# Every panel of seven products in block 1 opens with the two products that need no weight sums

## The chip, the cores and the metric

The kernel runs on one core of a Trainium2 chip. The metric is the time of one execution on the device in microseconds (us), as the median of several executions. All data are float32.

## The reference, cut to what matters

The reference chains two blocks over 256 tokens of width 1024. Block 1 has two layers; each is a hybrid mixer and a SwiGLU network. Block 2 (a gated recurrence, a retention mixer and two expert layers) is not touched by the change.

```
for l in range(2):
    proj = x @ w_in[l]            # 1024 x 6912: a_q a_k a_v | b_h b_b b_c | c_q c_k c_v | g_a g_b g_c
    y_a = sliding_window_attention(a_q, a_k, a_v)      # 8 heads of 64
    y_b = b_b * short_conv(b_c * b_h)
    y_c = moba_attention(c_q, c_k, c_v)                # 8 heads of 64, one block of 256 keys
    merged = sigmoid(g_a) * (y_a @ w_br_a) + sigmoid(g_b) * (y_b @ w_br_b) + sigmoid(g_c) * (y_c @ w_br_c)
    x = layer_norm(ALPHA * x + merged @ w_out)
    x = layer_norm(ALPHA * x + (silu(x @ w_gate) * (x @ w_up)) @ w_down)
```

## The kernel before, in words

**Panels.** The projections and the two up-projections of the feed-forward network are cut into panels of 1024 x 512 weights. A ring of six slots in SBUF receives them; SyncE (SP) issues the loads, each of which waits until TensorE has finished with the panel that held the slot. Each layer has 24 panels (`SEVENS`) that are multiplied by the x of 1024 x 256 with Strassen's scheme in Winograd's form: seven products of half-size blocks in place of eight.

**The seven products.** They are numbered 1 to 7. Products 1 and 2 read weights and x as they are. Products 5, 6 and 3 need sums of weight blocks (s1, s2, s4), and product 7 a difference that is written back into the panel; product 4 needs only sums of x, which are made once for many panels. VectorE makes the four sums in `weight_sums` (L2683, L2685, L2687, L2688). The three buffers for s1, s2, s4 exist once, so `weight_sums(q)` first waits until product 3 of panel q-1 is through (L2677: one semaphore step is given after product 3, L2331). For the first panel of the feed-forward run and the first gate panels after the first attention this wait is another one or none.

**PSUM.** The products go in pairs to four banks: A holds 5 and 6, B holds 3 and 7, C holds 1 and 2, D holds 4. `product_banks(q)` gives the order in which TensorE opens and fills them, the planner (`BankPlan`) numbers them, and VectorE waits for them. In panels 0, 4, 7, 9, 11 and 13 (`RUNS`, the first panels of runs) the order is C, A, B, D; in the other 18 it is A, B, C, D. Banks are handed out in turn: seven while one is held for the adaptive modulation's rows (up to the seventh feed-forward panel), then eight. A unit of work opens its bank as soon as the unit that used it before has emptied it.

**The combination.** ScalarE copies product 1 to SBUF (`first_product`, L2554) once bank C is full and the bank C before it is empty. VectorE then waits for that copy and all four banks and combines them in seven instructions (`parts`, L2699 to L2706). L2700 frees bank A, L2704 bank B, L2705 bank C and L2706 bank D.

**Order of work.** Each engine runs one list written by hand. TensorE in a layer: x transposed; panels 0 to 3 (b_h, b_b, b_c, a_q); a_k and a_v; eight scores (L2361, L2362); panels 4 to 6 (cq, ck, cv); eight scores; panels 7 and 8 (g_b); transposes and values of the first attention (L2246, L2406); the branch projection (L2263); panels 9 and 10 (g_a) and a branch; panels 11 and 12 (g_c), the second attention's values and a branch; the out projection (L2443); panels 13 to 23 (feed-forward); the down projection (L2501, L2509). VectorE, wherever it can, makes the sums of panel q+1 ahead of the combination of panel q. Between them stand logits (L2813), normalisations, the feed-forward product (L3009), and `ada_sums` (L2760, L2763), in which VectorE multiplies modulation weights. After panel 22 it makes the sums of the hidden rows (L3016 to L3019) and the first sums of the down weights (L3031 to L3034), and then combines panel 23.

Of the kernel before, what the change touches and what calls it, by code (L numbers as in the profile page):

```python
# [115 lines left out]
def view(ap, *dims):  # L116

    names = "abcd"[:len(dims)]
    return ap.rearrange(f"p ({' '.join(names)}) -> p {' '.join(names)}", **dict(zip(names[1:], dims[1:])))
# [10 lines left out]

FIRST = {"b": 0, "aq": 3, "cq": 4, "ck": 5, "cv": 6, "gb": 7, "ga": 9, "gc": 11, "ff": 13}
SEVENS = FIRST["ff"] + PAIRS
RUNS = (0, 4, 7, 9, 11, 13)


def product_banks(q):

    banks = (("A", (5, 6)), ("B", (3, 7)), ("C", (1, 2)), ("D", (4,)))
    return [banks[i] for i in (2, 0, 1, 3)] if q in RUNS else banks


STREAMS = 2
# [1721 lines left out]
def program(nc, I, K, out):  # L1864

    banks = BankPlan()
# [8 lines left out]
    def sevens(q, count=1):  # L1875
        steps = []
        for n in range(q, q + count):
            for name, _ in product_banks(n):
                steps += [("sv", n, name)] + [BankPlan.TICK] * (name == "A")
            steps += [R]  # L1880
        return steps
# [3 lines left out]

    layer = [(BankPlan.HOLD, BANKS - 1, ("adaG",))] + [("xT", t, m) for t in range(TT) for m in range(2)]
    layer += sevens(FIRST["b"]) + [("par",)] + sevens(FIRST["b"] + 1, 3)
    layer += [("ak",), ("av",), R, EV] + [("sa", h) for h in range(HEADS)]
    layer += sevens(FIRST["cq"]) + sevens(FIRST["ck"]) + [EV] + sevens(FIRST["cv"]) + [("sc", h) for h in range(HEADS)]
    layer += sevens(FIRST["gb"], 2) + attend("a") + branch("b") + [EV]  # L1890
    layer += sevens(FIRST["ga"], 2) + branch("a") + [EV]
    layer += sevens(FIRST["gc"], 2) + attend("c") + branch("c") + [EV]
# [19 lines left out]
    with ctx:  # L1912
# [72 lines left out]
        def middle(q):  # L1985
            return [view(a, 2, P) for a in M_PLACES[phase(q)]]
# [14 lines left out]
        def quarter_of(q, r, t):  # L2001

            if q == FIRST["cv"]:
                return view(cv[:, t, :], 2, 2, P)[:, :, r, :]
            return tiles_of(q)[:, :, r, P * t:P * t + P]
# [68 lines left out]
        def open_bank(pe, stage, key, i=0):  # L2074

            b = banks.bank(stage, key)
            pe.wait_ge(bank_free[b], banks.free(stage, key, i))
            return psum[:, b, :]

        def full_bank(eng, stage, key, i=0):  # L2080

            eng.wait_ge(pe_done, banks.full(stage, key, i))
            b = banks.bank(stage, key)
            return psum[:, b, :], bank_free[b]

        def wait_emptied(eng, stage, key, i=0):

            eng.wait_ge(bank_free[banks.bank(stage, key)], banks.emptied(stage, key, i))
# [142 lines left out]
        def _(pe):  # L2231
# [3 lines left out]
            def panel(i, width):  # L2235

                n = state["panel"]
                state["panel"] += 1
                per = state.get("per", 0)
                pe.wait_ge(panel_in[n % RING], i * (32 * per // RING) + 32 * (n // RING + 1))  # L2240
                return view(ring[:, n % RING, :], PANEL // width, width)
# [12 lines left out]
            for l in range(DEPTH):  # L2254
# [37 lines left out]
                def factor_pair(q, c, k, u, slot):  # L2292

                    w = view(slot[:, 4 * (c in (2, 4)) + k, :], 2, 2, P)[:, :, 1 if c in (4, 7) else 0, :]
                    left_made, right_made = left_sums(q), right_sums(q)
                    left = left_made[c][:, k] if c in left_made else w
                    if q != FIRST["cv"]:
                        left = left[:, u, :]
                    if c in right_made:
                        return left, right_made[c][:, k, :]  # L2300
                    return left, xT[:, 4 * (c in (2, 3)) + k, P * (c in (3, 5)):P * (c in (3, 5)) + P]

                def seven_products(q):

                    if q == 0 and l == 0:
                        pe.wait_ge(first_half_in, 16)
                        slot = view(ring[:, 0, :], KT, HALF)
                        state["panel"] += 1
                    else:
                        slot = panel(l, HALF)  # L2310
                    for name, two in product_banks(q):
                        bank = open_bank(pe, "layer", ("sv", q, name), l)
                        for j, c in enumerate(two):
                            if q == 0 and l == 0 and c == 2:
                                pe.wait_ge(panel_in[0], 32)
                            if c in (5, 6, 3, 7):
                                pe.wait_ge(sums_ready, 4 * (l * SEVENS + q) + {5: 1, 6: 2, 3: 3, 7: 4}[c])
                            if q == 0 and c in (5, 6, 7, 4):
                                pe.wait_ge(x_sums_ready, 8 * l + {5: 1, 6: 2, 7: 3, 4: 4}[c])
                            if q == FIRST["ff"] and c in (7, 5, 6, 4):  # L2320
                                pe.wait_ge(x_sums_ready, 8 * l + {7: 5, 5: 6, 6: 7, 4: 8}[c])
                            for k in range(4 if q == FIRST["cv"] else 0):
                                left, right = factor_pair(q, c, k, 0, slot)
                                last = mm(view(bank[:, SEQ * j:SEQ * j + SEQ], 2, P), right, left, start=k == 0, stop=k == 3)
                            for u in range(0 if q == FIRST["cv"] else 2):
                                for k in range(4):
                                    left, right = factor_pair(q, c, k, u, slot)
                                    a = SEQ * j + P * u
                                    last = mm(bank[:, a:a + P], left, right, start=k == 0, stop=k == 3)  # L2329
                            if c == 3:  # L2330
                                last.then_inc(pe_done, 1)  # L2331
                        last.then_inc(pe_done, 1)

                seven_products(FIRST["b"])
                pe.wait_ge(par_loaded, 4 * 16)
                pe.wait_ge(par_rest_loaded, 4 * 16)
                bank = open_bank(pe, "layer", ("par",), l)
                nc.tensor.transpose(bank[:, 0:128], par_rows, ident)
                nc.tensor.transpose(bank[:, 128:216], par2_rows[0:88, :], ident[0:88, 0:88]).then_inc(pe_done, 1)
                seven_products(FIRST["b"] + 1)  # L2340
                seven_products(FIRST["b"] + 2)
                seven_products(FIRST["aq"])

# [306 lines left out]
        def _(dve):  # L2650
# [16 lines left out]
            for l in range(DEPTH):  # L2667
# [22 lines left out]
                def parts(q):  # L2690

                    dve.wait_ge(first_ready, l * SEVENS + q + 1)
                    part, freed = {}, {}
                    for name, two in product_banks(q):
                        bank, freed[name] = full_bank(dve, "layer", ("sv", q, name), l)
                        for j, m in enumerate(two):
                            part[m] = view(bank[:, SEQ * j:SEQ * j + SEQ], 2, P)
                    one, sum_16, sum_165 = middle(q)
                    step(TTo(sum_16, one, part[6], ALU.add))  # L2699
                    TTo(sum_165, sum_16, part[5], ALU.add).then_inc(freed["A"], 1)  # L2700
                    wait_emptied(dve, "layer", ("sv", q, "A"), l)
                    TTo(quarter_of(q, 1, 1), sum_165, part[7], ALU.add)
                    step(TTo(sum_16, sum_16, part[7], ALU.add))
                    TTo(quarter_of(q, 0, 1), sum_165, part[3], ALU.add).then_inc(freed["B"], 1)  # L2704
                    TTo(quarter_of(q, 0, 0), one, part[2], ALU.add).then_inc(freed["C"], 1)  # L2705
                    TTo(quarter_of(q, 1, 0), sum_16, part[4], ALU.subtract).then_inc(freed["D"], 1)  # L2706
# [67 lines left out]
                step(V.tensor_copy(mods_0[:, :, :], mods_now[:, :, :]))  # L2774
                weight_sums(1)
                parts(0)
                bank, freed = full_bank(dve, "layer", ("par",), l)
                V.tensor_copy(par[:, :], bank[:, 0:128])
# [3 lines left out]
                step(V.tensor_copy(conv_w[:, :, :], view(par2[:, 64 + l * 12:76 + l * 12], 3, 4)))  # L2782
                weight_sums(2)
                parts(1)
                dve.wait_ge(cT_ready, l + 1)
                ada_sums(0, 0, 4)
                weight_sums(FIRST["aq"])
                parts(2)
                ada_sums(0, 4, KT)
                weight_sums(FIRST["cq"])  # L2790
# [368 lines left out]
```

## Time and profile before

| | |
|---|---|
| median of 3 executions | 2484.89 us (2484.7 to 2488.94) |
| profiled execution | 2485.11 us, span 2483.3 us |
| mean granted clock of TensorE | 0.961 of full |
| TensorE busy | 2188.5 us, 88% |
| VectorE busy | 1245.6 us, 50% |
| ScalarE busy | 369.2 us, 15% |

A view's busy time is the time in which an engine has at least one instruction in flight. A releaser (behind "<-") is the instruction that ended an idle time, as inferred from semaphores.

### The profile page before, as it was taken

What the parts mean: (1) busy time and instruction counts of PE and PEld (TensorE: products, weight loads), DVE (VectorE), ACT (ScalarE), POOL (GpSimd) and SP (SyncE); (2) the same over time, 40 slices, a digit from 0 to 9 for tenths busy, and PEclk for the clock granted to TensorE, in tenths of its full rate; (3) what the DMA queues carried; (4) which work ended last, traced back from release to release, by engine and by line L of the source; (5) the groups of instructions that cost most, each with busy time, mean ns of one, the idle gap of its engine ahead of it and who ended that gap; (6) DMA issues with size and microseconds to landing.
All of it is one profiled execution on the core that took longest, in us unless ns stands there. A gap on an engine that the chain in (4) does not pass through costs nothing.

```text
span 2483.3 us, 43563 instructions
## 1 busy us (share of the span) xinstructions
PE 2188.5 (88%) x19414; PEld 1578.0 (64%) x19414; DVE 1245.6 (50%) x2209; ACT 369.2 (15%) x825; POOL 38.5 (2%) x69
## 2 busy tenths in 40 slices
PE   8999999999999999999999988887799986565655
PEld 8998798499988984746545645454588543232322
DVE  7987787689777785926632222121444631111111
ACT  1121101012111001144430000000201420000000
POOL 0000000000000010000000000000000000000000
PEclk9999999999999999999999999999999998878787
DMA  9655765475558555401428999999920289999996
GB/s 321 238 170 187 247 195 221 155 269 207 190 192 276 191 205 189 161 28 35 160 104 333 426 426 426 426 426 426 366 102 34 95 339 426 426 428 426 428 427 289
DMA packets 168444, 659.16 MB, mean 265 GB/s; under 512 B 8358, under 2 KB 55970, under 8 KB 143554
## 3 DMA queue, kind: packets, MB, share of 16 engines
q1 hardware_dynamic: 162576, 639.66, 66.1%
q0 software_dynamic: 5312, 16.57, 2.1%
q8 instruction: 153, 2.51, 0.4%
q14 instruction: 33, 0.27, 0.0%
q10 hardware_dynamic: 370, 0.15, 0.0%
HBM read 655.12 MB, written 1.23 MB: 264 GB/s over the span
## 4 chain that ended last, share of the span: by engine, by line
PE 59%; DMA 28%; DVE 9%; ACT 2%; issue 1%; DVEq 0%; SPq 0%; ACTq 0%
PE psum L2329 20%; DMA ring<-in_moe_w_up 9%; DMA ring<-in_moe_w_gate 9%; DMA ring<-in_moe_w_down 9%; PE psum L789 5%; PE psum L538 4%; PE psum L2501 4%; PE psum L2263 3%; PE psum L715 3%; PE psum L806 2%; PE psum L2443 2%; PE psum L603 2%; PE psum L601 2%; PE psum L2509 1%; PE psum L859 1%
## 5 line engine op out<-in xcount | busy, mean ns | idle before, releaser
L789 PE MATMUL psum<-ring,arena 128*32 128x256 f32 x5888 | 383.1, 416 | 162.1 <-DMA ring<-in_moe_w_up 83.1
L789 PEld LDWEIGHTS psum<-ring,arena 128*32 128x32 f32 x5888 | 207.8, 118 | 334.3 <-issue 142.8
L1653 DVE TENSOR_TENSOR arena<-psum,spare 32x512 f32<-32x512 f32 (+1 forms) x128 | 70.9, 554 | 364.3 <-PE psum L806 363.0
L806 PE MATMUL psum<-ring,lnp 128*32 128x256 f32 x3072 | 192.5, 405 | 67.6 <-DMA ring<-in_moe_w_down 63.1
L806 PEld LDWEIGHTS psum<-ring,lnp 128*32 128x32 f32 x3072 | 103.6, 115 | 154.0 <-DMA ring<-in_moe_w_down 48.5
L1642 DVE TENSOR_TENSOR lnp<-arena,psum 128x512 f32<-128x512 f32 (+1 forms) x32 | 26.1, 816 | 326.4 <-PE psum L789 326.4
L2329 PE MATMUL psum<-ht,ring 128*128 128x128 f32 x1472 | 175.9, 278 | 2.3 <-DMA ring<-in_w_in 2.3
L2329 PEld LDWEIGHTS psum<-ht,ring 128*128 128x128 f32 x1472 | 170.8, 195 | 7.0 <-issue 7.0
L538 PE MATMUL psum<-ring,ht 128*128 128x512 f32 x320 | 140.6, 595 | 0.0
L1096 ACT ACTIVATE arena<-psum 128x512 f32<-128x512 f32 (+1 forms) x32 | 15.7, 491 | 669.2 <-PE psum L789 669.2
L2763 DVE SCALAR_TENSOR_TENSOR spare<-ring,arena,spare 128x512 f32<-128x512 f32 x168 | 113.8, 743 | 0.0
L538 PEld LDWEIGHTS psum<-ring,ht 128*128 128x128 f32 x320 | 59.9, 190 | 72.7 <-issue 72.5
L2329 PE MATMUL psum<-lnp,ring 128*128 128x128 f32 x768 | 92.0, 275 | 0.0
L2329 PEld LDWEIGHTS psum<-lnp,ring 128*128 128x128 f32 x768 | 88.8, 192 | 0.0
L2329 PE MATMUL psum<-c,ring 128*128 128x128 f32 x704 | 85.5, 275 | 0.0
L2263 PE MATMUL psum<-arena,ring 128*128 128x256 f32 x384 | 84.3, 380 | 0.9 <-ACT arena L2538 0.9
L2329 PEld LDWEIGHTS psum<-c,ring 128*128 128x128 f32 x704 | 82.0, 192 | 0.0
L2263 PEld LDWEIGHTS psum<-arena,ring 128*128 128x128 f32 x384 | 72.5, 190 | 11.4 <-ACT arena L2538 1.4
L715 PE MATMUL psum<-ring,arena 128*128 128x512 f32 x160 | 70.3, 594 | 1.8 <-DVE arena L1530 0.9
L2683 DVE TENSOR_TENSOR ht<-ring 128x1024 f32<-128x1024 f32 x39 | 47.7, 1223 | 45.4 <-PE psum L2329 44.1
L2329 PE MATMUL psum<-lnp,ht 128*128 128x128 f32 x512 | 60.0, 275 | 0.0
L2501 PE MATMUL psum<-ring,arena 128*128 128x512 f32 x128 | 57.7, 593 | 1.3 <-DVE arena L3034 1.3
(544 smaller groups left out, 3207.6 us busy)
## 6 DMA issues: line engine op xcount, KB each, us to landing
ring<-in_moe_w_down SPq DMA_DIRECT2D x64, 2048.0 KB
ring<-in_moe_w_gate SPq DMA_DIRECT2D x62, 2048.0 KB
ring<-in_moe_w_up SPq DMA_DIRECT2D x60, 2048.0 KB
ring<-in_w_in SPq DMA_DIRECT2D x51, 1024.0 KB, 8.9
ring<-in_ada_w SPq DMA_DIRECT2D x48, 1024.0 KB
ring<-in_w_ffn_gate SPq DMA_DIRECT2D x22, 1024.0 KB
ring<-in_w_ffn_up SPq DMA_DIRECT2D x22, 1024.0 KB
ring<-in_w_ffn_down SPq DMA_DIRECT2D x20, 1024.0 KB
```

The costliest lines, as they stand in the source:

```text
L538: last = mm(bank, lhs[:, k, P * t:P * t + P], slot[:, k, :], start=k == 0, stop=k == KT - 1)
L601: last = mm(out, left[:, part, :], right, start=k == 0, stop=k == 3)
L603: last = mm(out, right[:, P * part:P * part + P], left, start=k == 0, stop=k == 3)
L715: last = mm(bank, lhs[:, k, a:a + P], slots[n][:, k, :], start=k == 0, stop=k == KT - 1)
L789: last = mm(bank[32 * j:32 * j + 32, SPLIT * m:SPLIT * m + SPLIT], (x_last if layer else x_four)[:, k, e % 4, SLOTS * m:SLOTS * m + SLOTS] ...
L806: last = mm(bank[32 * j:32 * j + 32, SPLIT * m:SPLIT * m + SPLIT], hidT[:, e % 2, a:a + 32], slot[:, f % 4, SPLIT * j:SPLIT * j + SPLIT], ...
L1653: ins = TTo(y_four[32 * q:32 * q + 32, s0:, cols], view(bank[r, 0:width], len(src), SPLIT), gb_moe[r, s0:, cols], ALU.mult)
L2263: last = mm(bank[:, SEQ * h:SEQ * h + SEQ], slot[:, k, P * (2 * m + h):P * (2 * m + h + 1)], rhs[:, k, :], start=k == 0, stop=k == k_tiles ...
L2329: last = mm(bank[:, a:a + P], left, right, start=k == 0, stop=k == 3)
L2443: last = mm(bank, left, right, start=k == 0, stop=k == 3)
L2501: last = mm(down[c], left, right, start=i == 0, stop=False)
L2763: ins = STT(out=acc, in0=slot[:, k, :], scalar=weight, in1=acc, op0=ALU.mult, op1=ALU.add)
```

## The change

`product_banks` no longer takes the panel's number. It gives C, A, B, D for all 24 panels of a layer. The planner, TensorE and VectorE all ask it, so the order of filling, the numbering of the banks and the waits change together. The instructions and their number are the same. Panels 1, 2, 3, 5, 6, 8, 10, 12 and 14 to 23 change their order.

```diff
-RUNS = (0, 4, 7, 9, 11, 13)
-def product_banks(q):
+def product_banks():
     banks = (("A", (5, 6)), ("B", (3, 7)), ("C", (1, 2)), ("D", (4,)))
-    return [banks[i] for i in (2, 0, 1, 3)] if q in RUNS else banks
+    return [banks[i] for i in (2, 0, 1, 3)]
...
     def sevens(q, count=1):
-            for name, _ in product_banks(n):
+            for name, _ in product_banks():
                 steps += [("sv", n, name)] + [BankPlan.TICK] * (name == "A")
...
                 def seven_products(q):
-                    for name, two in product_banks(q):
+                    for name, two in product_banks():
                         bank = open_bank(pe, "layer", ("sv", q, name), l)
...
                 def parts(q):
-                    for name, two in product_banks(q):
+                    for name, two in product_banks():
                         bank, freed[name] = full_bank(dve, "layer", ("sv", q, name), l)
```

## Rows read from the trace of the kernel before

**Rows 1.** The page's busy times: us, share of the span, instructions.
```profile
PE 2188.5 (88%) x19414; PEld 1578.0 (64%) x19414; DVE 1245.6 (50%) x2209; ACT 369.2 (15%) x825; POOL 38.5 (2%) x69
```
**Rows 2.** Waits of TensorE: engine, line, releaser: us in total, times, longest.
```profile
PE psum L2406 <- DVE arena L2704: 3.1, 4, 0.8
...
PE psum L2501 <- DVE arena L3034: 1.3, 2, 0.7
...
PE psum L2361 <- DVE arena L2813: 0.9, 2, 0.5
...
PE psum L2361 <- DVE arena L2704: 0.6, 2, 0.3
```
**Rows 3.** Timeline of TensorE, panel 1: start, us, what, [idle before <-releaser].
```profile
26.32 3.77 PE L2329 MATMUL psum<-lnp,ht 128*128 128x128 f32 x32
...
31.72 1.95 PE L2329 MATMUL psum<-lnp,ring 128*128 128x128 f32 x16
...
38.86 3.74 PE L2329 MATMUL psum<-lnp,ht 128*128 128x128 f32 x32
```
**Rows 4.** Timeline of VectorE, the sums and combinations of panels 1 to 3.
```profile
32.02 1.23 DVE L2683 TENSOR_TENSOR ht<-ring 128x1024 f32<-128x1024 f32 x1 [1.02 <-PE psum L2329]
...
39.16 0.42 DVE L2699 TENSOR_TENSOR c<-c,psum 128x256 f32<-128x256 f32 x1 [2.27 <-PE psum L2329]
...
46.63 1.21 DVE L2683 TENSOR_TENSOR ht<-ring 128x1024 f32<-128x1024 f32 x1
...
51.67 0.42 DVE L2699 TENSOR_TENSOR c<-c,psum 128x256 f32<-128x256 f32 x1 [0.17 <-PE psum L2329]
```
**Rows 5.** Timeline of VectorE behind panel cv.
```profile
108.11 1.22 DVE L2683 TENSOR_TENSOR ht<-ring 128x1024 f32<-128x1024 f32 x1
...
114.26 0.42 DVE L2699 TENSOR_TENSOR c<-c,psum 128x256 f32<-128x256 f32 x1 [1.28 <-PE psum L2324]
...
116.30 0.41 DVE L2705 TENSOR_TENSOR arena<-c,psum 128x256 f32<-128x256 f32 x1
```
**Rows 6.** Timeline of TensorE: cq's end, ck, cv, the scores, panel 7.
```profile
84.80 3.74 PE L2329 MATMUL psum<-lnp,ring 128*128 128x128 f32 x32
88.53 3.81 PE L2329 MATMUL psum<-lnp,ht 128*128 128x128 f32 x32
...
101.77 3.72 PE L2324 MATMUL psum<-ht,lnp 128*128 128x256 f32 x16
...
116.43 0.48 PE L2361 MATMUL psum<-arena 64*128 64x128 f32 x2 [0.32 <-DVE arena L2704]
...
118.41 3.84 PE L2329 MATMUL psum<-ht,ring 128*128 128x128 f32 x32
```
**Rows 7.** Timeline of VectorE: the combination of panel 8 begins.
```profile
143.84 0.41 DVE L2699 TENSOR_TENSOR c<-c,psum 128x256 f32<-128x256 f32 x1
```
**Rows 8.** Timeline of TensorE: four groups of transposes, then attention values.
```profile
143.52 1.78 PE L2246 MATMUL psum<-const,arena 128*128 128x128 f32 x12
146.09 0.66 PE L2406 MATMUL psum<-arena 128*64 128x256 f32 x4 [0.79 <-DVE arena L2704]
```
**Rows 9.** Timeline of VectorE, feed-forward: sums of panel 23, combination of panel 22.
```profile
405.25 1.23 DVE L2683 TENSOR_TENSOR ht<-ring 128x1024 f32<-128x1024 f32 x1 [1.10 <-PE psum L2329]
...
410.05 0.68 DVE L3009 TENSOR_TENSOR arena<-arena 128x512 f32<-128x512 f32 x1
412.43 0.42 DVE L2699 TENSOR_TENSOR arena<-arena,psum 128x256 f32<-128x256 f32 x1 [1.70 <-PE psum L2329]
```
**Rows 10.** Timeline of TensorE in block 2: its two longest waits near 1300 us.
```profile
1298.47 0.41 PE L2246 MATMUL psum<-const,arena 128*64 128x128 f32 x2 [2.31 <-DVE arena L1556]
...
1305.59 0.67 PE L739 MATMUL psum<-arena,const 64*128 64x256 f32 x2 [3.27 <-DVE arena L1576]
```
**Rows 11.** Windows of core 0: us, busy by engine (instructions), PEclk, DMA share, GB/s.
```profile
1296.00:1300.00 4.00, 1.69 (x6) 0.82 (x6) 2.67 (x13) 3.60 (x4) 0.00 (x0) 1.00 1.00 369
...
1308.00:1312.00 4.00, 4.00 (x28) 4.00 (x27) 0.03 (x1) 1.24 (x4) 0.00 (x0) 0.71 0.10 41
```

## The prediction

> **What bounds the kernel now.** I read the page first, then the waits of TensorE, then the timelines of TensorE and VectorE side by side in block 1, and last the stretches where the granted clock falls. The page's first part puts TensorE at 88% of the span [rows 1]; the question is what holds it up in block 1, because only there does the edit act. The waits answer: in the two layers of block 1, TensorE stands still for VectorE in a few places, and they are short [rows 2]: one score (L2361) waits for the logits that empty its bank, another for the combination of panel cv, the attention values (L2406) wait for a bank that the last gate panel's combination empties, and the down projection (L2501) waits for its first weight sums. No product of L2329 waits for VectorE. So block 1 is bound by TensorE's own work, with VectorE just behind it at a few seams. Removing waits can return next to nothing; delaying VectorE at a seam costs in full.
>
> **The measure of the panel.** A panel of seven products takes 38.86 − 26.32 = 12.54 us; 16 of its 112 matmul records are one product. From 26.32 to 31.72 run products 5, 6, 3; from 31.72 to 38.86 run 7, 1, 2, 4 in 7.14 us [rows 3], so one is 1.785 and two are 3.57 us. The weight sums of panel q+1 (L2683 to L2688) overwrite the buffer that products 5, 6, 3 of panel q read, so they wait for product 3 of q. In the order A, B, C, D product 3 is third; in C, A, B, D it is fifth. **This is the main effect: on 18 of 24 panels of each layer, VectorE may begin the next weight sums 3.57 us later.** What it gives back: the next product 5 always comes four products after product 3; today, behind a run's first panel, only two.
>
> **Steady state, cost nothing.** After product 3 the new order leaves products 7, 4 and the next 1, 2: 4 x 1.79 = 7.1 us. Sum s1 is there after about 0.3 (the wait: 31.72 to 32.02 [rows 3, 4]) + 1.25 us. In the feed-forward run VectorE does per panel: sums 4.80 (405.25 to 410.05), the product of L3009 0.7, the combination (7 instructions, L2699 to L2706) 2.7 [rows 9], and in four panels 2.7 of adaptive sums: 10.9 us of 12.5. So VectorE keeps pace and its combination merely slides: now it waits 1.70 us for the panel's last product [rows 9]; then it starts 3.57 − 1.70 = 1.87 us later, or 1.9 with the spacing of two instructions back to back. Banks: the panel's first bank is now C, freed by the sixth instruction (L2705) instead of A, freed by the second. With seven or eight banks the next panel's last product is the first to need it, 10.7 us after the previous panel's end; it is free 1.9 + 2.5 us after. Covered. What I cannot read is a C-first panel in steady flow. Bounds: a run's first pair, C behind other work, takes 3.84 us against 3.74 for the same 32 records elsewhere [rows 6], so 0.10 x 36 panels = +3.6 us at most; nothing at least, since the same instructions run. I take zero: the 0.10 stands where another kind of work precedes.
>
> **Seam 1, the sliding-window scores.** VectorE is loaded here by adaptive sums. Panel 1: sums for panel 2 move from 32.02 to 35.59; its combination waited 2.27 us, so it starts at 40.39 instead of 39.16, +1.23. The following sums (46.63, no wait) would slide to 47.86; they wait for product 3 of panel 2 until 38.86 + 5 x 1.785 + 0.3 = 48.1, and the next combination goes from 51.67 to 48.1 + 4.8 = 52.9, +1.2. From there to the logits VectorE has no wait left, so they start 1.2 later too [rows 4]. The eighth score needs the bank of the first logit; it waits 0.9 / 2 = 0.45 us already [rows 2], so TensorE slips **+1.2 us**. What hid it today was those 2.27 us; that cover is gone.
>
> **Seam 2, the scores of the second attention.** Panels cq and ck follow. Product 5 of ck starts at 88.53, 3.73 us after product 7 of cq (84.80), where two products would take 3.57 [rows 6]: it waits for s1. With C first that is gone: −0.16, and −0.1 that follows it. So cv starts at 101.77 + 0.95 = 102.72 [rows 6]. In cv product 3 now ends five products in (5 x 1.75 = 8.75), at 111.5, and the sums behind it start at 111.7 instead of 108.11 [rows 5]. They take 4.80, so the combination of cv starts at 116.5 instead of 114.26 (it had waited 1.28). Second effect: the fourth score takes cv's first bank. Today that is A, and the fifth is the one that stands, for B, until 116.43 [rows 6]; then it is C, whose reader L2705 starts 2.04 after the combination's start (116.30 − 114.26) and takes 0.41 [rows 5], so 118.95, and the score starts at 119.0. Five scores remain, at (118.41 − 116.43) / 4 = 0.495 each: the gate panel starts at 121.5 instead of 118.41. **+3.1 us in all, of which 2.1 are new at this seam.**
>
> **Seams 3 and 4, the attention values.** The combination of the second gate panel starts at 143.84 and frees bank C by L2705, 2.04 + 0.41 us later [rows 5, 7]: 146.29. The fourth transpose group takes this bank now; a group takes 1.78 / 4 = 0.445. It starts at 146.35 and the values at 146.8 instead of 146.09 [rows 8]: **+0.7 us**. Rows 2 count four such waits (two per layer), so +0.7 again behind gc. The combination itself isn't late here: only the second panel of each pair changes its order, nothing in VectorE's queue waits for its product 3 sooner than today, and it starts with product D.
>
> **Seam 5, the down projection.** The last sums of the run start at 405.25 + 3.57; the combination of panel 22 at 412.43 + 1.9; then follow, with no wait between, the hidden sums and the first down sums, for which L2501 already waits 1.3 / 2 = 0.65 us [rows 2]. So **+1.9 us**. Behind it the down sums are ahead of TensorE again.
>
> **Other queues.** SP's panel loads wait for a panel's last product, which stays D; so do GpSimd's. They move with TensorE. ScalarE's copy of product 1 comes earlier and still waits for the former C bank; no combination waits for it.
>
> **Sum.** 3.06 + 0.72 + 0.72 + 1.91 = 6.4 us per layer, 12.8 for two (rows 2 count each seam equally in both). The profiled execution took 2485.11 us, 1.8 more than its span of 2483.3; the median of three is 2484.89. So 2485.11 + 12.8 − 0.2 = **2497.7 us**, +0.5%. The second block has no such panels and its streams start as its first panels come free, so it passes the shift on.
>
> **The rivals.**
> *A, the clock falls (2501).* The wait in seam 2 grows from 0.3 to some 2.5 us (three scores run from 102.72 + 12.3 = 115.0 to 116.5; the fourth starts at 119.0). In the second block a wait of 2.31 leaves the granted clock full; one of 3.27 us is followed by a stretch at 0.71 [rows 10, 11], part of it at 1.2 GHz, about (1 − 0.71) x 4 = 1.2 us, to which I add 0.5 for what may lie in the slice before. With 1.7 per layer: 2497.7 + 3.4. For it: 2.5 lies between. Against: it is nearer to 2.31. [...]
> *B, only the down projection is late (2489).* If VectorE's slack in the attention stage is more than the timeline shows (waits are rounded by the wait's own latency), seams 1 to 4 stay and 2 x 1.9 remain: 2484.9 + 3.8 = 2488.7. Against: rows 4 and 5 leave no gaps.
> *C, not slower (2483).* Behind each of the six run heads, product 5 comes two products after product 3 today. If each of these hand-overs costs the 0.16 seen at ck, in places that the waits don't name, the four products of cover give back 12 x 0.16 = 1.9 us: 2483.0. It decides if VectorE's sums, not its combination, are what TensorE meets next; the price is read at 88.53. Against it: the sums at ck are late because of adaptive sums, and elsewhere [rows 3] product 5 follows without a gap.
> *D, nothing moves (2485).* The slides of 1.2 to 1.9 us all die in waits of VectorE. For it: in the feed-forward run they do. Against: the four seams are places where TensorE waits for VectorE already.
>
> **How the numbers follow.** Forecast 0.74 (own range 2493.5 to 2501); A 0.09; B 0.07; C 0.05; D 0.05. About 0.2% (5 us) is what a measurement here tells from no change. B, D lie inside it, C too but may go beyond if the panels shorten; so slower 0.84, same 0.12, faster 0.04. The range 2491 to 2502 holds the forecast with a smaller seam 2 below, and rival A or the 0.10 per panel above.
>
> **What would show it.** The wait of L2361 for L2813 grows to 1.7 us each, that of L2361 for the combination to some 2.5 with L2705 as its releaser; L2246 waits for L2705 about 1 us before the values; L2501 waits 2.6; L2683 starts 3.57 later on changed panels; the feed-forward panels stay at 12.5. It is wrong if the feed-forward panels change length, if the waits above stay as they are, or if time goes or comes outside block 1.

## The result, and the profile after

| | before | changed |
|---|---|---|
| median | 2485.52 us (4 executions, 2484.7 to 2488.9) | 2509.14 us (4 executions, 2506.05 to 2512.78) |
| ratio | | 1.0093, 95% interval 1.008 to 1.0106 |
| profiled execution, span | 2485.11, 2483.3 us | 2512.78, 2511.0 us |
| mean granted clock | 0.961 | 0.952 |

The change makes the kernel 0.9% slower, 23.6 us. The forecast was 12.8 us. Line numbers of the changed kernel are one lower than those of the kernel before (L2328 is L2329).

The waits of TensorE in the changed kernel, in the columns of [rows 2]:

```profile
PE psum L2245 <- DVE arena L2704: 6.7, 4, 1.7
...
PE psum L2500 <- DVE arena L3033: 5.2, 2, 2.6
...
PE psum L2360 <- DVE arena L2704: 4.9, 2, 2.5
...
PE psum L2360 <- DVE arena L2812: 3.3, 2, 1.7
```

These are the same places as before and no new one, and each wait has grown: in order 1.67 for 0.79, 2.60 for 0.65, 2.48 for 0.32, 1.67 for 0.46 us. Where the kernel before waited for L2704 before the values, the changed one waits for the former L2705 before the fourth transpose group (here L2245 and L2704), and it is the fourth score, not the fifth, that stands in the second attention. The growth adds up to 14.2 us over two layers.

VectorE, timeline, where [rows 4, 5, 9] stood:

```profile
34.61 1.23 DVE L2682 TENSOR_TENSOR ht<-ring 128x1024 f32<-128x1024 f32 x1 [4.59 <-PE psum L2328]
...
39.41 0.42 DVE L2698 TENSOR_TENSOR c<-c,psum 128x256 f32<-128x256 f32 x1
...
112.43 1.23 DVE L2682 TENSOR_TENSOR ht<-ring 128x1024 f32<-128x1024 f32 x1 [4.11 <-PE psum L2323]
...
117.23 0.42 DVE L2698 TENSOR_TENSOR c<-c,psum 128x256 f32<-128x256 f32 x1
...
414.00 1.23 DVE L2682 TENSOR_TENSOR ht<-ring 128x1024 f32<-128x1024 f32 x1 [2.76 <-PE psum L2328]
...
419.52 0.42 DVE L2698 TENSOR_TENSOR arena<-arena,psum 128x256 f32<-128x256 f32 x1
```

The idle time has changed sides. Before, VectorE waited ahead of the combination (2.27, 1.28, 1.70); now it waits ahead of the sums (4.59 for 1.02 us in panel 1) and the combination follows with no wait. TensorE, timeline, at three of the places:

```profile
75.14 0.48 PE L2360 MATMUL psum<-arena 64*128 64x128 f32 x2 [1.67 <-DVE arena L2812]
...
75.99 5.46 PE L2328 MATMUL psum<-ht,ring 128*128 128x128 f32 x32
81.29 3.74 PE L2328 MATMUL psum<-lnp,ht 128*128 128x128 f32 x32
...
119.73 0.50 PE L2360 MATMUL psum<-arena 64*128 64x128 f32 x4 [2.48 <-DVE arena L2704]
...
432.57 3.75 PE L2500 MATMUL psum<-ring,arena 128*128 128x512 f32 x4 [2.60 <-DVE arena L3033]
436.12 3.20 PE L2500 MATMUL psum<-spare,arena 128*128 128x512 f32 x4
```

**Here stands what the forecast lacks.** The 32 records at 75.99 take 5.46 us, where the next 32 take 3.74; four records of L2500 take 3.75, later 1.88. The windows (us, busy of each engine, PEclk, DMA share, GB/s) show why:

```profile
76.00:78.00 2.00, 2.00 (x14) 2.00 (x14) 2.00 (x6) 0.00 (x0) 0.00 (x0) 0.74 1.06 392
78.00:80.00 2.00, 2.00 (x12) 2.00 (x11) 1.87 (x3) 0.00 (x0) 0.00 (x0) 0.50 1.05 386
80.00:82.00 2.00, 2.00 (x18) 2.00 (x18) 1.97 (x3) 0.43 (x2) 0.00 (x0) 0.91 1.05 386
...
151.00:153.00 2.00, 2.00 (x21) 1.43 (x18) 1.93 (x5) 1.41 (x4) 0.00 (x0) 1.00 1.05 407
...
434.00:436.00 2.00, 2.00 (x3) 0.67 (x2) 1.97 (x6) 0.15 (x1) 0.00 (x0) 0.50 1.04 422
```

Behind the wait TensorE works at 1.2 GHz (0.50 of 2.4) with as few as 12 records in a slice of 2 us that holds 20 or 21 at the full clock. The window at 151 us is the counterpart: the wait before the fourth transpose group ends at 149.82, is 1.67 us long like the one before the eighth score, and the clock behind it is 1.00. In the profile of the kernel before the clock stood at 1.00 from the first score to the end of both layers.

**A better yardstick.** Single executions of one kernel spread over 2 to 13 us. In the 14 profiles of this document, what lies behind block 1 takes 1505 to 1512 us, with no relation to the edits (1510.5 and 1505.3 in the two profiles of the changed kernel). So below I also give the **end of block 1**, the end of the last L2509: 959.57 + 18.02 = 977.6 us before, 982.51 + 18.02 = 1000.5 changed (+22.9), read from the chain of waits. The **clock's loss** is the sum of (1 − PEclk) x 10 us over slices of 10 us of both layers, from the first score to the last down product: 0 before, 10.2 us changed. It comes in steps of 1.7: one near 77 us, two near 433, one near 575, one near 620, one near 935.

### The profile page after: what moved, and what is told of

Its sections match the earlier page's. It is cut to its first block, busy times and chain, and to the rows that moved or that the text cites. A ratio compares the mean times of both kernels' runs of the same rounds, so it can differ in the third digit from the quotient of the medians.

```text
span 2511.0 us, 43599 instructions
## 1 busy us (share of the span) xinstructions
PE 2204.9 (88%) x19414; PEld 1585.7 (63%) x19414; DVE 1246.5 (50%) x2209; ACT 366.7 (15%) x825; POOL 38.7 (2%) x69
## 4 chain that ended last, share of the span: by engine, by line
PE 60%; DMA 27%; DVE 9%; ACT 2%; issue 1%; DVEq 0%; SPq 0%; ACTq 0%
PE psum L2328 21%; DMA ring<-in_moe_w_gate 9%; DMA ring<-in_moe_w_up 9%; DMA ring<-in_moe_w_down 9%; PE psum L788 5%; PE psum L2500 4%; PE psum L537 4%; PE psum L2262 3%; PE psum L714 3%; PE psum L805 2%; PE psum L2442 2%; PE psum L600 2%; PE psum L602 2%; PE psum L2508 1%; PE psum L2245 1%; PE psum L818 1%
## 5 line engine op out<-in xcount | busy, mean ns | idle before, releaser
L2328 PE MATMUL psum<-ht,ring 128*128 128x128 f32 x1472 | 179.5, 282 | 3.1 <-DMA ring<-in_w_in 2.2
L2328 PEld LDWEIGHTS psum<-ht,ring 128*128 128x128 f32 x1472 | 173.8, 197 | 8.4 <-issue 8.1
L2328 PE MATMUL psum<-lnp,ring 128*128 128x128 f32 x768 | 89.7, 275 | 0.0
L2328 PEld LDWEIGHTS psum<-lnp,ring 128*128 128x128 f32 x768 | 87.7, 192 | 0.0
L2328 PE MATMUL psum<-c,ring 128*128 128x128 f32 x704 | 82.2, 275 | 0.0
L2328 PEld LDWEIGHTS psum<-c,ring 128*128 128x128 f32 x704 | 80.4, 192 | 0.0
L2500 PE MATMUL psum<-ring,arena 128*128 128x512 f32 x128 | 60.1, 613 | 5.2 <-DVE arena L3033 5.2
L2328 PE MATMUL psum<-lnp,ht 128*128 128x128 f32 x512 | 59.8, 275 | 0.0
```

What stands on the lines that cost most here:

```text
L2500: last = mm(down[c], left, right, start=i == 0, stop=False)
```

## The experiments

The main theory: late weight sums and a late bank C lengthen five waits per layer (the forecast), and the clock's fall behind them is the rest. Where a kernel has other orders than the change, it is built from the kernel before by its list `RUNS` of panels with C first.

### The change again

> The change as it is, repeated. Theory (T): the predicted waits of TensorE are all there (in the profile of the changed kernel 1.67, 2.48, 1.67 twice and 2.60 us per layer, where the kernel before had 0.46, 0.32, 0.79 twice and 0.67), which explains some 13 to 14 us of the +23.6; the rest is TensorE's granted clock, which falls to half for 1.4 to 3 us behind the first score wait and behind the down projection's wait in both layers. So T expects +19 to +27 us, the spread of the runs larger than before. Rival (R): the extra 10 us came from block 2 or from the chip of that day; then this run is near +13.

Measured: 2507.71 us against 2488.14, ratio 1.0091 (1.0073 to 1.0108), +19.6 to +22.6 us by medians and ratio. The waits are the same to 0.1 us. Block 1 ends at 999.2; the clock's loss is 8.5 us. So the result holds, and the extra 10 us lie in block 1. The loss differs between two profiles of the same program, 10.2 and 8.5. It isn't a matter of the profiled executions alone: each execution has a mean granted clock, 0.951 to 0.956 in these six and 0.952 to 0.962 in the fifteen of the kernel before. (1 − clock) x time is 115 us on average here and 105 there, 10 us more, to some 3 us by their scatter.

### Feed-forward panels alone

```diff
-RUNS = (0, 4, 7, 9, 11, 13)
+RUNS = (0, 4, 7, 9, 11, 13, 14, 15, 16, 17, 18, 19, 20, 21, 22, 23)
```

> Only panels 14 to 23 (feed-forward) change their order; the attention stage is as before. T expects the down projection's wait alone: 2 x 1.9 us of wait plus a clock drop of 1.7 and 3.1 us as in the changed kernel's profile: +8 to +9 us. Rival W (waits alone, the clock's loss is elsewhere): +3.8 us. Rival N (the feed-forward panels themselves run slower in this order): more than +10.

Measured: ratio 1.0017 (1.0007 to 1.0027), +4.2 us; block 1 ends at 984.35, +6.8, of it 3.4 the clock's. By time rival W is nearer, by the profile theory T: in this profile both layers fall, and the ten executions reach from 2488.7 to 2495.8. Their mean loss of clock, (1 − clock) x time, is 105 us as in the kernel before, so the two falls of this profile don't show in the average. TensorE, timeline, of this kernel:

```profile
427.07 2.53 PE L2501 MATMUL psum<-ring,arena 128*128 128x512 f32 x4 [2.59 <-DVE arena L3034]
429.40 3.04 PE L2501 MATMUL psum<-spare,arena 128*128 128x512 f32 x4
432.28 5.31 PE L2501 MATMUL psum<-ring,arena 128*128 128x512 f32 x12
```

The panels 16 to 19 take 50.03 us in the kernel before, the changed one and this one: a panel opening with C has no price of its own, as the forecast took it.

### All but panel 22

```diff
+RUNS = tuple(q for q in range(24) if q != 22)
```

> The change, but panel 22 alone keeps A, B, C, D, so that the sums of panel 23 start after the third product of panel 22. T: the lateness at the down projection comes from this one hand-over, so it all goes: 8 to 9 us less than the changed kernel of the same call, +14 to +16 us against the kernel before. Rival (the lateness has piled up over ten panels): nothing changes, +23.

Measured: ratio 1.0071 (1.0053 to 1.0089); block 1 ends at 991.7. The down projection, timeline of TensorE:

```profile
430.95 1.95 PE L2501 MATMUL psum<-ring,arena 128*128 128x512 f32 x4 [0.68 <-DVE arena L3034]
432.74 1.88 PE L2501 MATMUL psum<-spare,arena 128*128 128x512 f32 x4
```

One hand-over decides: with panel 22 as before, the wait is back at 0.68 and the 112 records of L2501 take 48.3 instead of 49.8 to 51.4 us, although all 23 other panels open with C. The lateness does not pile up over ten panels. By the yardstick 7.5 us are gone, by time 2.4 of a pair of medians whose ranges overlap.

### Filling the wait of the down projection

```diff
+                    if d == 0:
+                        warm = open_bank(pe, "layer", ("dn", SEVEN[0]), l)
+                        for _ in range(5):
+                            mm(warm[:, 0:SEQ], hid[:, 0, 0:P], slots[0][:, 0, 0:SEQ], start=True, stop=True)
                     pe.wait_ge(w_sums_ready, l * 6 + (d + 1))
```

> The change, with five matmuls of 256 columns more per layer (about 5 x 0.43 = 2.15 us of TensorE work whose result is overwritten) inside the 2.6 us in which TensorE waits for the first down sums. No dependency changes. T: the wait is not shorter, but TensorE does not rest, the clock stays at 1.00 and the following matmuls take 1.72 per four instead of up to 3.55: 4 to 5 us less than the changed kernel of the same call. Rival (the clock's fall is not caused by the rest): no difference, or a little slower by the matmuls themselves.

Timeline of TensorE (the filling is L2498) and the window behind it:

```profile
430.41 2.32 PE L2498 MATMUL psum<-ring,arena 128*128 128x256 f32 x10
432.96 1.98 PE L2505 MATMUL psum<-ring,arena 128*128 128x512 f32 x4 [0.22 <-DVE arena L3038]
434.78 1.88 PE L2505 MATMUL psum<-spare,arena 128*128 128x512 f32 x4
```
```profile
434.00:436.00 2.00, 2.00 (x6) 0.87 (x5) 1.93 (x6) 0.00 (x0) 0.00 (x0) 1.00 1.03 422
```

At this place T holds in both layers: same sums, same dependency, clock at 1.00, 48.3 us. The Trainium skill, "TensorE: Matmul & The Clock Gate", section "HAM oscillation — how this bites in real kernels" (HAM is its name for the clock gate), warns of idle gaps in matmul work. The trace agrees in kind, since only the rest was taken away; it doesn't in size, for the gaps named there are longer than the 2.6 us that did it here. Yet the time is not better: ratio 1.0089 (1.0074 to 1.0103), and block 1 ends at 996.65, 2.5 us sooner than in the repeated change. A new fall stands at the layer's end, near 508 us (1.7 us of loss). So the expectation on the total fell.

### Panels 1, 2 and 3 as before

```diff
+RUNS = (0,) + tuple(range(4, 24))
```

> The change, but panels 1, 2 and 3 keep A, B, C, D. The yardstick is the end of block 1 in the profile (the last L2509: 977.6 us in the kernel before, 999.2 in the repeated change). T: the wait of L2361 for the logits goes from 1.67 back to 0.46 in both layers, 2.4 us, and the clock stays full over panels 4 and 5 (25.2 instead of 26.5 and 26.8 us), 2.9 us more: block 1 ends near 994. Rival (the clock's fall over panels 4 and 5 belongs to the panels, not to the wait before them): 2.4 us less alone, near 997.

Waits of TensorE in this kernel:

```profile
PE psum L2501 <- DVE arena L3034: 5.2, 2, 2.6
...
PE psum L2361 <- DVE arena L2705: 4.9, 2, 2.5
...
PE psum L2361 <- DVE arena L2813: 1.3, 2, 0.8
```

Measured: ratio 1.007 (1.0053 to 1.0086); block 1 ends at 993.6 (expected 994). The first score wait is 0.79 us in layer 0 and 0.47 in layer 1. Panels 4 and 5 take 25.21 us in both layers instead of 26.5 and 26.8. The first score wait is due to the late sums of panels 1 to 3, and the clock's fall over panels 4 and 5 to that wait. At 25.21 they are also 0.23 us faster than before the change (25.44): this is the short hand-over at ck which the forecast had credited with 0.26.

### Panel 6 as before

```diff
+RUNS = tuple(q for q in range(24) if q != 6)
```

> The change, but panel 6 (cv) alone keeps A, B, C, D. T: the wait at the fourth score goes from 2.48 to some 0.3 at the fifth, 2.1 us per layer: block 1 ends near 995, and 1 us less where the clock had fallen behind it. Rival (the sums before, of panels 4 and 5, are what makes VectorE late here): less than 1 us in both layers together.

```profile
PE psum L2361 <- DVE arena L2813: 3.3, 2, 1.7
...
PE psum L2361 <- DVE arena L2704: 0.6, 2, 0.3
```

Measured: ratio 1.0053 (1.0036 to 1.007); block 1 ends at 992.45. The second score wait is that of the kernel before. From the start of cv to panel 7 it is 16.64 us in this kernel and in the kernel before, 18.49 in the repeated change: **1.85 us per layer is the price of this one panel**, where the forecast had 2.1.

### Bank C freed early

```diff
                     step(TTo(sum_16, one, part[6], ALU.add))
+                    TTo(quarter_of(q, 0, 0), one, part[2], ALU.add).then_inc(freed["C"], 1)
                     TTo(sum_165, sum_16, part[5], ALU.add).then_inc(freed["A"], 1)
...
-                    TTo(quarter_of(q, 0, 0), one, part[2], ALU.add).then_inc(freed["C"], 1)
```

> The change with its order of filling, but VectorE's combination makes the quarter that reads bank C as its second instruction instead of its sixth; instructions and count are the same. It tells the two effects apart, the banks' order and the late sums. T: the waits of L2246 (1.67, four of them) vanish, since bank C is free 0.9 us after the combination's start; at the fourth score 1.2 us per layer go, until the first logit is the limit; the first score wait and the down projection's stay as they are, since they come from late sums: 9 us less, block 1 ends near 990. Rival (the waits of L2246 come from a late combination, not from the order in which it frees banks): the four waits stay above 1 us and block 1 ends above 996.

Waits of TensorE (L2700 now frees C, L2705 B):

```profile
PE psum L2501 <- DVE arena L3034: 5.2, 2, 2.6
PE psum L2361 <- DVE arena L2813: 3.3, 2, 1.7
...
PE psum L2361 <- DVE arena L2700: 1.8, 2, 0.9
...
PE psum L2246 <- DVE arena L2705: 0.9, 4, 0.2
```

Measured: ratio 1.0043 (1.0027 to 1.0059), half of the change's loss, by moving one instruction; block 1 ends at 986.7 (expected 990). The attention values' waits were the bank order alone (1.67 to 0.2), the fourth score's was order and lateness together, and the other two, from late sums, stay to the tenth. The clock did not fall behind the two waits of 2.6 us here, which neither theory expects.

### Filling the first score wait

```diff
                     for h in range(HEADS):
+                        for _ in range(3 if (kind, h) == ("a", HEADS - 1) else 0):
+                            mm(psum[:, banks.bank("layer", ("adaG",)), SEQ:2 * SEQ], xT[:, 0, 0:P], xT[:, 0, :],
+                               start=False, stop=False)
                         bank = open_bank(pe, "layer", (f"s{kind}", h), l)
```

> The change with three matmuls of 256 columns more per layer (about 1.3 us of TensorE work whose result nobody reads) inside the 1.67 us wait before the eighth score of the sliding window. T: the panel 4 still starts as late, but the clock stays full over panels 4 and 5: 25.2 instead of 26.5 to 26.8 us, block 1 ends 2.5 to 3 us sooner, near 996. Rival (the fall is not tied to the rest before it): no difference.

```profile
73.17 1.56 PE L2360 MATMUL psum<-ht 128*128 128x256 f32 x6
74.91 0.48 PE L2364 MATMUL psum<-arena 64*128 64x128 f32 x2 [0.17 <-DVE arena L2816]
...
75.75 3.84 PE L2329 MATMUL psum<-ht,ring 128*128 128x128 f32 x32
```

Measured: ratio 1.0073 (1.0057 to 1.009); block 1 ends at 997.3. Panels 4 and 5 take 25.21 in both layers, so the fall at this place goes with the rest. Falls stand elsewhere: at the down projection in both layers, and near 118 us (fourth score) and 787 us, where the repeated change had none.

### The kernel before with a later VectorE

```diff
+                TTo(view(arena[:, 14336:15360], 4, SEQ), bh, bh, ALU.mult)
                 TTo(yb, yb, bb, ALU.mult).then_inc(yb_ready, 1)
```

> The kernel before, orders untouched, with one VectorE instruction more per layer (1024 columns, about 1.2 us, its result unread) ahead of the logits of the first attention. It makes the wait of L2361 for L2813 as long as in the changed kernel, 1.67 instead of 0.46 us, without any change of order. T: the clock falls here as well, panels 4 and 5 take 26.5 to 26.8 instead of 25.4 us, and block 1 ends 2 x (1.2 + 1.2) = 4.8 us later than 977.6, near 982. Rival (the fall needs the new order of products): 2.4 us later alone, near 980, panels 4 and 5 at 25.2.

Wait and windows of this kernel:

```profile
PE psum L2361 <- DVE arena L2814: 3.2, 2, 1.6
```
```profile
76.00:78.00 2.00, 2.00 (x14) 1.82 (x13) 2.00 (x6) 0.00 (x0) 0.00 (x0) 0.75 1.06 394
78.00:80.00 2.00, 2.00 (x11) 2.00 (x11) 1.87 (x4) 0.00 (x0) 0.00 (x0) 0.50 1.05 388
```

Measured: ratio 1.0016 (1.0007 to 1.0026); block 1 ends at 981.0. In layer 0 panels 4 and 5 take 26.84 us, with no order changed; in layer 1, behind the same 1.62 us, 25.44. So **the wait brings the fall about, not the new order, and it doesn't do so every time.**

### Filling two places, and five

The first kernel has the two fillings shown above at once, the eighth score's of the first attention and the down projection's.

> The change with the filling matmuls at both places, before the eighth score and before the down projection. T: nearly no fall of the clock is left in block 1, and what remains against the kernel before are the waits alone, the forecast's own sum: block 1 ends 13 to 14 us after 977.6, at 991 to 992. Rival (a cost that neither waits nor clock show): it ends above 994.

Measured: ratio 1.0082 (1.0067 to 1.0098). At the two filled places the clock stays full in both layers; block 1 ends at 996.4 and the expectation falls, since 6.8 us of clock loss stand at places that were left: 1.7 and 3.4 at the fourth score of layers 0 and 1, and 1.7 behind the second attention's transposes in layer 0:

```profile
238.00:240.00 2.00, 2.00 (x11) 1.30 (x11) 1.97 (x2) 1.00 (x3) 0.00 (x0) 0.50 1.03 414
240.00:242.00 2.00, 2.00 (x18) 1.37 (x16) 1.97 (x2) 1.10 (x3) 0.00 (x0) 0.73 0.99 380
```

The second fills all five, the down projection's as above:

```diff
+                        fill({("a", 7): 3, ("c", 3): 5}.get((kind, h), 0))
...
+                            fill(3 if n == 3 else 0)
                             transposes("layer", key, [probs[:, h, P * m:P * m + P] for m in range(3)], l)
```

> The change with filling matmuls at all five places where TensorE waits longer than before: three of 256 columns before the eighth score, five before the fourth score of the second attention (2.15 of 2.48 us), three before the fourth transpose group of each attention (1.3 of 1.67 us), five before the down projection. In the kernel with filling at two places the clock fell at the other three instead, and block 1 ended at 996.4, not at the 991 to 992 expected. T: with nothing left to fall behind, the clock stays at 1.00 through both layers up to the out projection and from there to the down projection, and block 1 ends at 991 to 993, 13 to 15 us after 977.6: the waits alone, the forecast's sum. Rival (a third cost beside waits and clock, or fillings that cost as much as they save): it ends at 995 or later with the clock at 1.00.

Its waits, and two windows of layer 1:

```profile
PE psum L2246 <- DVE arena L2717: 1.5, 4, 0.4
...
PE psum L2513 <- DVE arena L3046: 0.5, 2, 0.2
...
PE psum L2368 <- DVE arena L2825: 0.4, 2, 0.2
```
```profile
500.00:600.00 100.00, 99.79 (x904) 95.71 (x897) 90.23 (x151) 17.15 (x56) 0.00 (x0) 1.00 0.71 256
600.00:700.00 100.00, 99.51 (x727) 90.34 (x726) 79.39 (x119) 18.95 (x54) 0.00 (x0) 1.00 0.52 170
```

Measured: 2499.22 us against 2487.08, ratio 1.0045 (1.0031 to 1.0059), +11.2 us; block 1 ends at 987.8, +10.2. The clock's loss in the two layers is zero. All of VectorE's lateness is still there; only TensorE no longer rests in it. This halves the loss, from 1.0091 to 1.0045, by adding work. It ends 3 us below the expectation; some 2 us are issue gaps in the stretch from the out projection to panel 13 and at the layer's end, which are there in one profile and not in the next. By the five executions (1 − clock) x time is 106 us on average against 105 in the kernel before, where the repeated change had 10 us more. Whether filling the four transpose waits was needed is not shown: left unfilled, they brought one fall in 32 cases.

### Banks freed in the order in which they are wanted

Built from the kernel before, which has waits of this kind too:

```diff
+LAST_GATES = (8, 12)
...
+    if q in LAST_GATES:
+        return [banks[i] for i in (0, 2, 1, 3)]
...
                     wait_emptied(dve, "layer", ("sv", q, "A"), l)
+                    early = q in LAST_GATES
+                    if early:
+                        TTo(quarter_of(q, 0, 0), one, part[2], ALU.add).then_inc(freed["C"], 1)
...
                         ff_product(p - 1)
+                    if p == 9:
+                        ada_columns()
                     parts(FIRST["ff"] + p)
```

> Built from the kernel before, not from the change. Panels 8 and 12 are filled in the order A, C, B, D and their combination frees C as its third instruction, so that the banks come free in the order in which the transposes and values of the attention ask for them; and the copy of the adaptive columns moves into the 1.7 us in which VectorE waits before the combination of panel 22. T: the four waits of L2406 (0.79 each) vanish and the wait of L2501 falls from 0.67 to 0.25: 4 us less, block 1 ends near 973.6, 2484 where the kernel before has 2488 (ratio 0.998). Rival: the next bank, B, is then the one waited for, and half of it is left, 975.5.

```profile
PE psum L2364 <- DVE arena L2710: 0.6, 2, 0.3
PE psum L2504 <- DVE arena L3041: 0.5, 2, 0.2
```

Measured: 2485.73 us against 2488.09, ratio 0.9989 (0.998 to 0.9998); block 1 ends at 974.1 (expected 973.6). The four waits before the attention values are gone, that of the down projection is 0.25. The gain is small, 2.4 us by the medians and 3.5 by the yardstick. The kernel is faster than both others.

## Why the prediction was wrong

**Right: the mechanism and the places of the waits.** The forecast named five places and their releasers, with sizes of 1.7, some 2.5, about 1 (twice, before the values) and 2.6 us. Measured: 1.67, 2.48, 1.67 twice, 2.60. The wait before the values was named too short; its own rows give 146.35 − (143.52 + 3 x 0.445) = 1.5. The cost it put there, 0.72 us, came as 0.7, because the old wait of 0.79 behind the transposes is gone. Its sum can be read in the kernel with five fillings, where the clock plays no part. Counted from panel 1, in layer 0 the start of panel 4 is (77.09 − 26.54) − (75.83 − 26.49) = 1.2 us later, as forecast; panel 7 is 2.8 later (3.06), the branch projection 3.6 (3.8), its second counterpart 4.3 (4.5). Layer 1 is 6.0 us longer in all (6.4), so two layers of waits cost some 12 us where the sum has 12.8. One term was a little too large, seam 2 by 0.25.

**Right: what costs nothing.** Feed-forward panels at 12.51 us, no wait in them, the upper bound of 0.10 per panel not needed; the late sums of panels 14 to 21 are absorbed in VectorE's own waits. The credit at ck (0.26) came as 0.23.

**Wrong: the clock.** The step that failed is the sum's silence on it: what TensorE's clock would do behind the longer waits was put at nothing. Rival A's rule failed too: that of the grown waits only seam 2's would count, because "a wait of 2.31 leaves the granted clock full; one of 3.27 us" does not. That read a threshold from two waits of another stretch, and the trace of the kernel before already had a third wait against it, just behind block 1 (timeline of TensorE, then windows):

```profile
985.49 5.54 PE L2246 MATMUL psum<-const,arena 128*128 128x128 f32 x32 [1.79 <-issue]
```
```profile
984.00:988.00 4.00, 2.51 (x14) 2.54 (x15) 2.66 (x10) 3.10 (x6) 0.00 (x0) 0.75 1.05 388
```

A wait of 1.79 us, shorter than 2.31, and the clock's mean falls to 0.75 in the 4 us around its end. This same wait, which no edit touches, is followed by a fall in 6 of the 14 profiles. In block 1 the clock fell at the first score wait, only 1.6 to 1.7 us long, in 12 of 14 cases (seven profiles, two layers each), at the down projection's 2.6 in 11 of 14, and at seam 2's 2.5 us in 9 of 14. At the equally long 1.67 us before the fourth transpose group it fell in 1 of 32. In the changed kernel that makes 10.2 and 8.5 us of loss in its two profiles, to some 12 to 14 from the waits: 20 to 24 together, against the measured +23.6 and +19.6. The term was put at 0 in the forecast and at 3.4 in rival A. A came nearest, in kind, and a third of the size; it had a chance of 0.09.

**Rivals B, C, D.** B and D fall with the waits; the seams have no hidden slack. C's gain exists where it was read (0.23 at ck) and nowhere else.

**What stays open.** What decides whether a particular wait is followed by a fall. The falls in block 1 begin between 0.8 us before and 2.0 us after the end of the wait. Behind each of the 18 filled waits of four kernels (the down projection's in two layers, the first score's in two, both of these, all five) the clock stayed full, but it may fall at an unfilled one instead. Length alone doesn't decide: 1.67 us before the eighth score brought a fall in 12 of 14 cases, before the transposes in 1 of 32, and an unfilled 1.52 us before the eighth score in layer 0 of the last kernel brought none. Whether the clock depends on how light the work before the wait is (the scores use 64 of 128 rows) wasn't tried, nor was filling only the three places where most falls stood (32 of 35 in block 1). Nor did the times resolve each edit of 2 us; those rest on profiles, one for each kernel.

## What to carry to other kernels

Where one engine is at work without a break, cost a new wait twice: its length, and the slower clock that may follow; here some 12 us of waits became 20 to 24. Before changing the order in which products are made, ask two things of the engine behind: which buffer is released by the product that now comes later, and whether banks still come free in the order in which the next stage wants them. If a wait can't be removed, harmless matmuls in it may be worth more than they look. Here filling one or two of five places showed no gain in time that could be told from noise; filling all five halved the loss.

## What the runs showed of the hardware that was not expected

- TensorE's granted clock fell to 0.50 at waits from 1.6 us on in work that is otherwise dense. Of 35 falls in block 1 of 14 profiles, 31 cost about 1.7 us and four 3.4. A wait of 2.31 us in block 2 left the clock full [rows 10, 11], and two waits of 2.6 did so in one kernel.
- The same wait in the same place is followed by a fall in one profile and not in another (1.79 us just behind block 1: 6 of 14), and waits of one length differ by place (1.67 us: 12 of 14 before the eighth score, 1 of 32 before the transposes).
- With two places filled, 6.8 us of loss stood at others; with five filled, none.
- With 19 more matmuls of 256 columns in each layer (3 and 5 in the score waits, 3 and 3 ahead of the transposes, 5 in the down projection; some 0.43 us each, 8 us per layer) the changed kernel took 2499.22 us, without them 2507.71, each in its own set of runs, with ratios of 1.0045 and 1.0091. TensorE had more to do and ended sooner.
